# Moving the by-count weight rows ahead, and the first two weight splits behind the first pick, in two expert stages of a 24,000-instruction kernel

## The reference, cut to what matters

```python
def moe(h2, router_w, router_b, w1, w3, w2):
    scores = jax.nn.sigmoid(h2 @ router_w)                  # 256 tokens x 16 experts
    biased = (scores + router_b).reshape(n_tok, 4, 4)       # 4 groups of 4 experts
    gidx = jnp.argmax(jnp.sum(lax.top_k(biased, 2)[0], -1), -1)   # best group
    ...                                                     # its 2 best experts: eid
    gates = sel / jnp.sum(sel, axis=-1, keepdims=True)
    ...                                                     # the tokens of each expert are gathered
    y = (jax.nn.silu(xb @ w1[e]) * (xb @ w3[e])) @ w2[e]    # 1024 -> 512 -> 1024, f32
    ...                                                     # y * gate is added at the token's row
```

## Time and profile before

| | us |
|---|---|
| median of 3 runs | 2023.87 |
| lowest and highest | 2021.21, 2025.34 |
| span of the profiled execution | 2024.2 |
| TensorE busy in it | 1860.4 (92%) |
| VectorE busy | 1115.7 (55%) |
| ScalarE busy | 761.4 (38%) |
| share of TensorE in the chain that ended last | 71% |
| share of VectorE in that chain | 18% |
| mean granted TensorE clock | 0.959 |

### The profile page before, as it was taken

How to read it: one execution, slowest core, us unless ns; L and a number is a source line. 1 busy time by engine, 2 the same in 40 slices (tenths; PEclk the granted TensorE clock), 3 DMA queues, 4 the chain that set the end, 5 groups by cost and what they waited for, 6 DMA issues and landing times.

```text
span 2024.2 us, 24328 instructions
## 1 busy us (share of the span) xinstructions
PE 1860.4 (92%) x9824; PEld 1322.0 (65%) x9824; DVE 1115.7 (55%) x1863; ACT 761.4 (38%) x1203; POOL 94.8 (5%) x136
## 2 busy tenths in 40 slices
PE   6998899999899899999989897999999798889997
PEld 5655565454576555556735575888888574579997
DVE  5672532233444432345557727788766755756665
ACT  2163243333241332334236625323222334654443
POOL 0780000000000000000000000000000100000000
PEclk8989899999899999999989998999999997989998
DMA  8768399999556799995210021345445131024440
GB/s 359 304 280 337 146 392 400 414 397 407 212 210 268 291 417 420 421 419 200 96 63 1 1 82 43 137 177 206 190 184 208 42 118 49 1 84 173 182 146 22
DMA packets 61865, 430.17 MB, mean 213 GB/s; under 512 B 6576, under 2 KB 9776, under 8 KB 9904
## 3 DMA queue, kind: packets, MB, share of 16 engines
q1 hardware_dynamic: 61744, 428.51, 53.4%
HBM read 427.43 MB, written 1.05 MB: 212 GB/s over the span
## 4 chain that ended last, share of the span: by engine, by line
PE 71%; DVE 18%; ACT 9%; issue 2%; DMA 0%; DVEq 0%; SPq 0%; ACTq 0%
PE bank L293 14%; PE bank L1141 10%; PE bank L297 9%; PE bank L298 9%; PE bank L299 9%; PE bank L1129 7%; DVE ring_halves L2467 2%; PE bank L332 2%; ACT work_halves L2461 2%; ACT work_halves L1061 2%; PE bank L2140 1%; DVE ring_halves L1068 1%; PE bank L2117 1%; DVE work L439 1%; PE bank L2491 1%
## 5 line engine op out<-in xcount | busy, mean ns | idle before, releaser
L297 PE MATMUL bank<-work_halves 128*128 128x512 f32 (+1 forms) x1344 | 472.0, 351 | 30.9 <-DVE HH_halves L2759 15.1
L299 PE MATMUL bank<-work_halves,ring_halves 128*128 128x512 f32 (+1 forms) x1344 | 460.7, 343 | 0.0
L297 PEld LDWEIGHTS bank<-work_halves 128*128 128x128 f32 x1344 | 258.1, 192 | 68.5 <-DVE HH_halves L2759 16.2
L298 PE MATMUL bank<-HH_halves,work_halves 128*128 128x512 f32 (+1 forms) x832 | 288.8, 347 | 0.0
L299 PEld LDWEIGHTS bank<-work_halves,ring_halves 128*128 128x128 f32 x1344 | 258.0, 192 | 28.8
L1141 PE MATMUL bank<-ring,work 128*64 128x512 f32 x1024 | 261.2, 598 | 0.4 <-ACT work_halves L1324 0.4
L2467 DVE TENSOR_TENSOR ring_halves<-ring,work_halves 128x2048 fp32r<-128x2048 f32 x72 | 164.7, 2287 | 51.0 <-ACT work_halves L2461 51.0
L298 PEld LDWEIGHTS bank<-HH_halves,work_halves 128*128 128x128 f32 x832 | 161.1, 194 | 20.3 <-issue 2.2
L293 PE MATMUL bank<-HH,ring 128*128 128x256 f32 x704 | 161.9, 390 | 13.2 <-DVE HH L518 6.6
L298 PE MATMUL bank<-work_halves 128*128 128x512 f32 (+1 forms) x512 | 172.0, 336 | 0.0
L293 PEld LDWEIGHTS bank<-HH,ring 128*128 128x128 f32 x704 | 136.5, 196 | 43.0 <-issue 13.8
(11 more groups left out here) (325 smaller groups left out, 2611.6 us busy)
## 6 DMA issues: line engine op xcount, KB each, us to landing
ring<-in_ws_dram SPq DMA_DIRECT2D x380, 1024.0 KB, 7.3
work<-in_ws_dram SPq DMA_DIRECT2D x24, 1024.0 KB, 9.7
con<-in_con_dram SPq DMA_DIRECT2D x1, 1204.0 KB, 25.0
XX<-in_xT_dram SPq DMA_DIRECT2D x1, 1024.0 KB, 9.8
XX<-in_cT_dram SPq DMA_DIRECT2D x1, 1024.0 KB, 15.3
out_dram<-XX SPq DMA_DIRECT2D x2, 512.0 KB, 3.2
par<-in_par_dram SPq DMA_DIRECT2D x1, 338.0 KB, 2.9
con<-in_con_dram SPq DMA_DIRECT2D x1, 128.0 KB, 2.8
```

Source lines behind the costliest of these rows:

```text
L297: pe.matmul(out, l[0], r[0], start=start, stop=False)
L298: pe.matmul(out, l[0], r[1], start=False, stop=False)
L299: return pe.matmul(out, l[1], r[0], start=False, stop=stop)
```

## The change

Three moves on DVE, the same in both expert stages. No instruction is added or removed; the other engines' lists are the same but for line numbers.

- `order_rows` goes from behind the token rows to right behind the permutation, inside `order`.
- "places" goes from ahead of `order` to behind `order_rows`.
- `split_dve(0, 1)` goes from ahead of `route` to behind `pick(0)`.

```diff
@@ route
                 st.wait_ge(dve, "ranks")
-                dve.scalar_tensor_tensor(out=pq, in0=bP[:, 0:32], scalar=1.0, in1=mask, op0=ADD, op1=MUL).then_inc(st.dve("places"), 1)
                 self.order(dve)
@@ order
                 st.wait_ge(dve, "perm")
+                self.order_rows(dve)
+                bP = bank[5]
+                dve.scalar_tensor_tensor(out=self.pq, in0=bP[:, 0:32], scalar=1.0, in1=self.mask, op0=ADD, op1=MUL).then_inc(st.dve("places"), 1)
                 st.wait_ge(dve, "places")
                 self.by_round(dve, self.pq, self.pqh, "place")
@@ dve
-                self.split_dve(dve, 0, 1)
                 self.route(dve)
                 reg = self.load_count(dve)
                 self.pick(dve, 0)
+                self.split_dve(dve, 0, 1)
                 st.wait_ge(dve, "rows", 3)
                 for i in range(4):
...
                 for i in (*self.steps[1], *self.steps[2]):
                     self.bg.dve(dve, i)
-                self.order_rows(dve)
                 self.by_round(dve, self.gate, self.gateh, "gate")
```

## The result

| | before | after |
|---|---|---|
| median, us | 2023.94 (4 runs, 2021.21 to 2025.34) | 2034.01 (4 runs, 2031.15 to 2035.24) |
| span of the profiled execution | 2024.2 | 2033.5 |
| ratio to before, 95% interval | | 1.0050 [1.0036, 1.0064] |

The changed kernel is slower by 10.1 us, with 7.3 to 13.0 as the interval; 10.2 were forecast. The runs of one kernel spread over 4 us, so that the two numbers agree to 0.1 us is chance.

What follows compares the result with a forecast made beforehand. TensorE's time was taken to bound the body, with transfers following. Gather delays of 5.2 and 3.9 us plus 1.1 us of clock sum to 10.2 us, for a 2034.1 us median; own range 2031 to 2037, 8-in-10 range 2027.5 to 2038.

Steps and rivals of the forecast that it cites:

- Splits off the front gain nothing: Ahead of route on DVE: scores or TensorE's background chunks hold the chain anyway, so its start behind the ranks stays; 0 us.
- Splits ahead of the token rows, +4.4 us each: Between pick and token rows on DVE: two splits delay the token rows, and so TensorE's gather, by 4.41 us per stage.
- order_rows and places, +1.28 us on the chain: Ahead of the picks on DVE: counts, place halves and pick all come 1.28 us later in each stage.
- The weights 6.6 us earlier "gain nothing": SP's weight stream resumes 6.6 us sooner, but TensorE doesn't wait for these chunks; 0 us.
- comes later by the same 1.28: TensorE's branch ahead of the gather: shifts by 1.28 us, letting the gather begin at 252.4 and 674.7.
- 1.97 - 0.14 us beyond the token rows: Second stage's head before the change: TensorE's branch read as ending 1.8 us later than the token rows' pick-up.
- The clock, +1.1 in the second stage and 0 in the first: TensorE's gather after longer idle: 1.1 us slower in the second stage, +0 in the first; bounds -1.1 and +3.
- The transfers as the bound: Rival for both bodies: the HBM stream lasts longest, so each stage ends 6.6 us earlier, 2010.7 us; 4%.
- Part won back in the body: Rival: TensorE's 3.4 and 1.9 us waits are for late chunks, removed by an earlier stream; 2028.8 us, 7%.
- The splits hide: Rival at the head: TensorE's branch or something unnamed holds the gather, covering the 5.69 us; 2024.5 us, 5%.
- A new wait behind the gather: Rival: DVE's branch ends late, splits 2 and 3 delay w3 of round 0; 2 to 4 us more, 2037, 14%.

Runs made afterwards that it cites:

- e1: The kernel before with only the two splits (0, 1) moved from ahead of route to behind the first pick; ratio 1.0019 [1.0007, 1.0030].
- e3: The kernel before with order_rows moved later, from ahead of the gates' sum to behind the four memsets; ratio 1.0002 [0.9989, 1.0016].
- e4: The kernel before with order_rows moved much later, behind DVE's splits 2 and 3; ratio 1.0069 [1.0046, 1.0091].
- e6: The changed kernel with the two splits one step later, behind the four token rows; ratio 1.0022 [1.0011, 1.0032].
- e7: The kernel before with token rows ahead of the ranks, counts ahead of the permutation, count load and then splits behind the first pick; ratio 0.9992 [0.9982, 1.0002].
- e10: e7 with order_rows right behind the permutation, so weights stream inside TensorE's branch; ratio 1.0004 [0.9993, 1.0014].
- e11: The changed kernel with SP holding later rounds' weight chunks until TensorE's first gather product; ratio 1.0051 [1.0035, 1.0066].
- e2: The changed kernel with its splits put back ahead of route, so only order_rows and places are moved; ratio 1.0029 [1.0017, 1.0041].
- e9: e2 with SP holding later rounds' weight chunks until TensorE's first gather product; ratio 1.0017 [1.0008, 1.0027].

## Why the prediction was right, and what in it was wrong

**Splits off the front gain nothing: right in the profiles of before, after and e1, but not always.** In after the ranks' counting matmul (L1190) follows TensorE's background chunks without a gap, and DVE waits 2.46 us for it, as it waited 2.41. e1 shows the same. The premise that the ranks wait for TensorE holds only where TensorE's work ahead of them is slow. In e3 and e4, whose splits stand in front, the background chunks of the first stage ran at a granted clock of 1.00, route began 1.14 us behind the scores, and TensorE waited for the mask (e3):

```profile
238.38 0.39 PE L1190 MATMUL bank<-work,con 128*128 128x16 f32 x2 [1.20 <-DVE work L1487]
```

In the first stages of e6, e7, e10 and e11, at the same clock but with nothing in front, this wait is 0.11 us. So the move can give back 1.1 us ahead of the ranks in some executions, and the heads of the table, which begin at L1190, leave that out.

**Splits ahead of the token rows, +4.4 us each, of which the branch covers a part: right.** They take 4.40 us in after. Alone, beside a branch that came no later, they were to cost 3.9 and 2.6 us, and e1 measures 3.93 and 2.60 from ranks to gather.

**order_rows and places, +1.28 us on the chain: right for DVE.** After has 247.35 - 241.00 = 6.35 us from ranks to pick, before 247.34 - 242.27 = 5.07. As a change of its own it costs more (e2), for the next reason.

**The weights 6.6 us earlier "gain nothing": right for the body, wrong for the head.** e3, e4 and e11 show that the body needs no earlier stream. But the earlier stream also has a price that I put at nothing: it lengthens the branch by 2.6 and 1.2 us in the changed kernel, 2.8 and 1.4 in e2. The step that failed is that the branch on TensorE "comes later by the same 1.28" and would let the gather begin at 252.4 and 674.7. It took a length from a stretch with a nearly idle DMA into one where the change makes DMA busy. The absolute times don't compare, since the second stage begins later in after, so count from the ranks: the forecast is 10.1 and 11.2 us. In truth the branch ends 12.4 and 11.5 us behind the ranks and would let the gather begin at 12.7 and 11.7, 2.6 and 0.5 us later than forecast. In the second stage the error is small because two things nearly cancel: the branch is 1.2 us longer, but begins only 0.6 us later, since in before TensorE's background work had kept it until 669.1, past the counts (667.83). The total came out right since the gather, held by the token rows, comes at 14.06 and 13.83 us, later still by 1.4 and 2.1 us. That is luck as far as the branch goes. Had the splits stood one place later (e6), the same working would have said +2.6 us where 4.5 [2.2, 6.5] were measured, and where the heads alone grew by 6.2.

The branch had also been inferred as "1.97 - 0.14 us beyond the token rows" when its own row could be read: 3.94 us from 669.2, to 673.1, with the gather at 673.40.

**The clock, +1.1 in the second stage and 0 in the first: 1.1 and -0.8 in the profile, so +0.3 and not +1.1.** It lies within the bounds. The second stage's gather did take 6.67 us. But over the kernels the gather behind an idle time of 8 to 14 us takes anything from 5.40 (e11, second stage, 8.2 us idle) to 6.73 us (e11, first stage, 13.7 us idle), and the same 13.7 us gave 5.88 in after. Which it is depends on where in the gather the granted clock rises from 0.50 to 1.00: 3.1 us behind its start in the first of these, 6.1 in the second, 4.2 in the third. It is a spread of 1.3 us per stage and no term, and that the second stage gave 1.1 is luck.

**Rivals.** The transfers as the bound: refuted by e2, e3 and e11. Part won back in the body: TensorE's waits are the same 3.4 and 1.9 us, and from round 0 to round 3 it takes the same 32.8 us in both stages. The splits hide: e1. A new wait behind the gather: not there; DVE's idle time before splits 2 and 3 is 4.51 and 5.19 us, released by ACT.

## What to carry to other kernels

A wait for several things hides the lengths of all but the last; when a change delays one, work out the others' new lengths too, and not only their new starts. An instruction moved earlier on one engine starts transfers earlier, and they may run into a neighbour's fetch of code: read the queue for instructions and the branch's own row before calling early transfers free. And idle time on a waiting engine is worth filling only up to the work that must follow within it: the splits were hidden, or all but hidden, ahead of the scores and exposed behind them.

## What the runs showed of the hardware

A branch on TensorE over a long skipped block took 3.3 to 3.9 us with under 70 GB/s moving in the mean of the branch, and 5.1 to 6.3 us with weights streaming at 317 to 418 GB/s in its first 3 us. e9 against e2 and e11 against after show that the stream is the cause. That it acts through the fetch of the code behind the branch is borne out by the packets on q8: the branch ends 1.3 to 1.5 us behind the one 16 KB packet, wherever that falls, and under the stream the packet begins 2.8 to 4.0 us in, not 0.9 to 1.5. Why the packet begins late no run shows. In two places (4.8 and 5.1 us, e7 and e4) the branch was long with no more moving (under 40 GB/s), and two such packets ran side by side; that is a second way to a long branch, seen and not tested.

The Trainium skill, Runtime: NRT & Kernel Launch, section "Instruction fetch mechanics", says that a taken branch out of the loaded pages forces a DMA fetch before execution goes on. The trace agrees, with the branch ending 1.3 to 1.5 us behind the packet; the stall's length and its growth under load are what these rows add.

On ACT and DVE the same branch shows 0.04 and 0.06 us in its own row, so this view alone doesn't tell what such a branch costs there; ACT's table load came 2.5 us after it in before (249.86), and that was not followed up.
